# Diagonal blocks of the differential scores: a minimum on VectorE in place of mask products on TensorE

## The reference, cut to what matters

```
causal = key_pos[None, :] <= q_pos[:, None]
z = jnp.einsum('bhqcd,bhkcd->bhcqk', qi, k).astype(jnp.float32) * scale
z = jnp.where(causal, z, -jnp.inf)
probs = jax.nn.softmax(z, axis=-1)
a = probs[:, :, 0] - lam * probs[:, :, 1]
return jnp.einsum('bhqk,bhkd->bhqd', a.astype(v.dtype), v)
```

## Time and profile before

| | |
|---|---|
| median of the runs shown | 1189.08 us |
| the profiled execution's own time | 1189.23 us |
| its span | 1187.4 us |
| TensorE products, busy | 1177.8 us (99%) |
| TensorE weight loads, busy | 985.2 us (83%) |
| VectorE, busy | 830.1 us (70%) |
| ScalarE, busy | 719.6 us (61%) |
| GpSimd, busy | 95.8 us (8%) |
| products with `mask_df` | 16, from 284.1 to 916.1 us |
| granted clock of TensorE, mean | 0.999 |

### The profile page before, as it was taken

How to read it: one execution, slowest core, us unless ns; L and a number is a source line. 1 busy time by engine, 2 the same in 40 slices (tenths; PEclk the granted TensorE clock), 3 DMA queues, 4 the chain that set the end, 5 groups by cost and what they waited for, 6 DMA issues and landing times.

```text
span 1187.4 us, 17137 instructions
## 1 busy us (share of the span) xinstructions
PE 1177.8 (99%) x6032; PEld 985.2 (83%) x6032; DVE 830.1 (70%) x1198; ACT 719.6 (61%) x1162; POOL 95.8 (8%) x158
## 2 busy tenths in 40 slices
PE   9999999999999999999999999999999999999997
PEld 7888888888788888888888888878877888888886
DVE  6766767577667766676787776775766777767666
ACT  7655556766665755555685655576556666555554
POOL 5000001042000000000100000010600000000001
PEclk9999999999999999999999999999999999999999
DMA  8656565654345565656556555746343456556550
GB/s 286 220 184 205 178 212 181 198 175 139 113 174 177 178 207 182 203 171 218 177 167 205 174 198 187 242 160 213 121 148 132 168 177 211 178 178 209 180 194 36
DMA packets 138638, 215.36 MB, mean 181 GB/s; under 512 B 6942, under 2 KB 97888, under 8 KB 138592
## 3 DMA queue, kind: packets, MB, share of 16 engines
q1 hardware_dynamic: 135792, 208.43, 52.2%
q10 hardware_dynamic: 2576, 6.29, 1.7%
q0 software_dynamic: 224, 0.04, 0.0%
HBM read 213.68 MB, written 1.05 MB: 181 GB/s over the span
## 4 chain that ended last, share of the span: by engine, by line
PE 99%; DMA 0%; DVE 0%; ACT 0%; DVEq 0%; POOLq 0%; issue 0%; POOL 0%; ACTq 0%
PE ps L1544 22%; PE ps L1426 20%; PE ps L1428 19%; PE ps L1427 19%; PE ps L1554 12%; PE ps L1473 1%; PE ps L1645 1%; PE ps L1678 1%; PE ps L1691 1%; PE ps L1664 0%; PE ps L1651 0%; DMA soft<-in_p 0%; PE ps L1707 0%; PE ps L1704 0%; PE ps L1714 0%; PE ps L1722 0%
## 5 line engine op out<-in xcount | busy, mean ns | idle before, releaser
L1069 DVE SCALAR_TENSOR_TENSOR w_lo<-raw,g_layer,w_hi 128x512 fp32r<-128x512 f32 (+1 forms) x524 | 388.0, 800 | 139.3 <-ACT w_hi L632 138.6
L632 ACT ACTIVATE w_hi<-raw,g_layer 128x512 fp32r<-128x512 f32 (+1 forms) x524 | 346.9, 732 | 113.4 <-PE ps L1554 97.0
L1544 PE MATMUL ps<-x_both,w_hi 128*128 128x512 f32 x1152 | 287.7, 392 | 0.0
L1426 PE MATMUL ps<-w_hi,x_both 128*128 128x512 f32 x640 | 258.6, 404 | 0.1
L1428 PE MATMUL ps<-w_hi,x_both 128*128 128x512 f32 x640 | 250.5, 391 | 0.0
L1427 PE MATMUL ps<-w_lo,x_both 128*128 128x512 f32 x640 | 249.7, 390 | 0.0
L1544 PEld LDWEIGHTS ps<-x_both,w_hi 128*128 128x128 f32 x1152 | 209.3, 189 | 39.4 <-issue 0.3
L1066 DVE TENSOR_TENSOR w_lo<-raw,w_hi 128x1024 fp32r<-128x1024 f32 x114 | 134.7, 1222 | 55.3 <-ACT w_hi L629 55.3
L629 ACT ACTIVATE w_hi<-raw 128x1024 fp32r<-128x1024 f32 x114 | 114.7, 1052 | 91.9 <-PE ps L1428 91.8
L1554 PEld LDWEIGHTS ps<-x_both,w_lo 128*128 128x128 f32 x1152 | 152.6, 191 | 8.4
L1554 PE MATMUL ps<-x_both,w_lo 128*128 128x256 f32 x1152 | 156.0, 283 | 0.0
(11 more groups left out here) (216 smaller groups left out, 977.0 us busy)
## 6 DMA issues: line engine op xcount, KB each, us to landing
raw<-in_ffn_w_gu SPq DMA_DIRECT2D x170, 512.0 KB, 4.5
raw<-in_ffn_w_down SPq DMA_DIRECT2D x88, 512.0 KB, 3.9
raw<-in_w_in SPq DMA_DIRECT2D x80, 512.0 KB, 4.5
raw<-in_w_out SPq DMA_DIRECT2D x16, 512.0 KB, 4.0
raw<-in_w_ple_gate SPq DMA_DIRECT2D x16, 512.0 KB, 4.0
raw<-in_w_branch_sb SPq DMA_DIRECT2D x8, 512.0 KB, 3.7
raw<-in_w_branch_diff SPq DMA_DIRECT2D x8, 512.0 KB, 3.7
raw<-in_ffn_w_gu SPq DMA_DIRECT2D x12, 256.0 KB, 7.8
```

What stands on the lines that cost most here:

```text
L632: last = act.activation(w_hi[:, s, part], raw[:, s, part], ACT.Copy, scale=g_layer[:, g:g + 1])
L1069: last = dve.scalar_tensor_tensor(out=w_lo[:, s, part], in0=raw[:, s, part], scalar=g_layer[:, g:g + 1], in1=whi[:, part], op0=ALU.mult, o ...
L1426: pe.matmul(dst, x_h, w_h, start=first, stop=False, **group)
L1544: mm = pe.matmul(dst, w_hi[:, s, cols], x_both[:, :, 4 * half + k, :], start=half == 0 and k == 0, stop=stop and k == 3, skip_group_check= ...
```

## The change

The two mask products of each head are gone; the first score product of each bank now carries start=True and begins the bank. VectorE, once the scores are there, takes the elementwise minimum of the two diagonal blocks of each bank with a block of caps: 3.0e38 where the key may be seen, -1.0e30 where it may not. These are two instructions a head (one a bank) on 128x256 numbers, read from PSUM and written back in place. The maxima then wait for the second one by a semaphore of VectorE's own (`d_capped`). At the start GpSimd makes one 128x128 block of caps in float32 in place of two bf16 mask blocks.

```diff
-        mask_df = sb("mask_df", [P, SEQ], BF16)
+        cap_df = sb("cap_df", [P, 1, P])
...
-            pool.memset(mask_df[:, :], 0.0).then_inc(blank, 1)
+            pool.memset(cap_df[:, :, :], BIG).then_inc(blank, 1)
...
-
-                last = pool.affine_select(out=mask_df[:, c:c + P], in_=mask_df[:, c:c + P],
-                                          compare_op=ALU.is_ge, fill=NEG, base=0, pattern=[[-1, P]],
-                                          channel_multiplier=1)
-            last.then_inc(const_all, 1)
+            pool.affine_select(out=cap_df[:, 0, :], in_=cap_df[:, 0, :], compare_op=ALU.is_ge, fill=NEG, base=0,
+                               pattern=[[-1, P]], channel_multiplier=1).then_inc(const_all, 1)
...
                         dve.wait_ge(d_score, DF_HEADS * i + hd + 1)
+                        for c in range(2):
+                            last = dve.tensor_tensor(diagonal(DF_BANK[c]), diagonal(DF_BANK[c]),
+                                                     cap_df[:, :, :].to_broadcast([P, 2, P]), ALU.min)
+                        last.then_inc(d_capped, 1)
+                        dve.wait_ge(d_capped, DF_HEADS * i + hd + 1)
                         for t, (lo, hi) in enumerate(((0, P), (P, 384))):
                             last = dve.tensor_reduce(neg_max[:, t::2], ps[:, 6:8, lo:hi], AX_X, ALU.max, negate=True)
                         last.then_inc(d_max, 1)
...
-                for c in range(2):
-                    masked(DF_BANK[c], mask_df)
                 for c, rows in enumerate(HEAD_ROWS):
-                    pe.matmul(bank(DF_BANK[c])[:, 0:P], dfq_t[rows, hd, 0:P], dfk_t[rows, hd, 0:P], start=False,
+                    pe.matmul(bank(DF_BANK[c])[:, 0:P], dfq_t[rows, hd, 0:P], dfk_t[rows, hd, 0:P], start=True,
                               stop=False, skip_group_check=True)
```

More of the change, by code:

```diff
@@ L26 @@
 NEG = -1.0e30
+BIG = 3.0e38
 TT = SEQ // P
@@ L240, in trunk_kernel @@
         d_score = sem("d_score")
+        d_capped = sem("d_capped")
         d_max = sem("d_max")
```

## The result

The changed kernel takes 1192.61 us (median of 8 runs, 1192.47 to 1192.74) against 1189.05 us (8 runs, 1188.90 to 1189.27): +3.56 us, ratio 1.0030, 95% interval 1.0021 to 1.0038. The prediction was 1192.6. The profiled execution took 1192.47 us with a span of 1190.5. One execution of the second experiment took 2726 us and one of the kernel before beside it 3212 us, where the others took 1193 and 1189; the ratios leave both out.

A forecast was written before the change was run, and what follows sets the result against it. TensorE is 99% busy, but the prediction took the head-to-head chain across four engines to decide: D added per head, less absorption and freed masks, gives 2 x 1.76 = +3.5 us, 1192.6 us; range 1190.0 to 1195.0.

The forecast's parts named there:

- D: VectorE, each head: two minima and the wait start the maxima 0.78 us later; bounds 0.45 and 1.30.
- head 1, load for the values: TensorE, layer 0: the load waits for ScalarE's `mixed_t` and comes at 311.54 instead of 310.76, +0.78 us.
- head 2, load for the values: TensorE, layer 0: load comes at 326.85, in time for its product but no longer early, costing 0.10 us.
- head 3, load for the scores: TensorE, layer 0: load waits for the scaled output, at 331.02 instead of 330.15, +0.87 us.
- head 3, load for the turn: TensorE, layer 0: load waits for `mixed`, at 337.99 against 337.24 by its own pace; TensorE at +1.49 us.
- last turn, load: TensorE, layer 0: load waits for the scaled output, at 344.77 instead of 342.97; TensorE at +1.76 us.
- Where it is absorbed and where not: Layer 0's chain: head 0 absorbs D, its squares unmoved; later heads pass it on, TensorE ending +1.76 us.
- What is removed: TensorE: eight mask blocks at 0.32 us each give 2.6 us; bounds 0.21 and 0.42 a block.
- Twice 1.76 us: Both layers: each is 1.76 us later at its last turn, +3.5 us in all.
- the cover: Rival: minima fall in VectorE's idle time and TensorE keeps its 2.6 us, 1186.5 us; chance 0.07.
- The dearer minimum: Rival, VectorE: writing to PSUM makes D 1.0 to 1.3, +5.3 to +7.7 us, 1195.6 us; chance 0.11.
- less late: Rival: D nearer 0.5 or one more link TensorE had held, +0.5 to +2.3 us, some 1190.6; chance 0.22.

The follow-up runs named there:

- the second experiment: The kernel before with its masks kept on TensorE, and the two minima and their wait added on VectorE: 1193.24 us (ratio 1.0040).
- the three mended moves: Changed kernel with squares before the high pass's second half, earlier copies for heads 1 and 3, maxima between low-pass halves, `os_lo` before head 1's minima: 1186.31 us.
- the mended pair: The same mended moves on the changed kernel, 1186.31 us, and on the kernel before with masks on TensorE, 1188.47 us.

## Why the prediction was right, step by step

The trace after starts 0.34 us lower at the last product ahead of head 0's scores, where the mixing block has not changed yet (283.58 against 283.92, the fences below). The 0.34 us are there in the first 10 us, behind the first wait for the program's input, 0.41 us in this trace and 0.73 in the other; over the kernels above the same product stands anywhere from 283.09 to 283.92, so I count it as no part of the change. With 0.34 added to the times after:

| step | predicted | measured |
|---|---|---|
| minima and wait, D | 0.78 | 0.80 at head 0, 0.79 at head 1 |
| head 1, load for the values | 311.54 | 311.60 |
| head 2, load for the values | 326.85 | 326.92 |
| head 3, load for the scores | 331.02 | 331.13 |
| head 3, load for the turn | 337.99 | 338.06 |
| last turn, load | 344.77 | 344.82 |

The times fall 0.05 to 0.11 us behind the forecast ones. That the total agreed to 0.01 us is closer than its steps and luck in the last digit; the path is as forecast.

- *The addition D.* Right by the nearest row; a write to PSUM cost VectorE no more than one to SBUF (0.42 us, as `os_lo`). The rule of the Trainium skill (VectorE: DVE Perf Modes, The DRAIN you can't avoid) that a wait costs nothing extra gave 0.66 and +2.5 us; this case's trace does not agree: the maxima begin 0.04 us behind the second minimum's end (284.87 + 0.76 to 285.67), not 0.09 before it.
- *Where it is absorbed and where not.* Head 0 absorbs it, and with that its slack is used up; heads 1 to 3 do not. The experiment that puts the same time behind `mixed` and the one that keeps the masks both confirm it; that the whole loss is this chain is shown by the three mended moves, which take it away with the minima in place.
- *What is removed.* This term was mis-sized, with little effect on the total (by the prediction's own bounds 0.1 us or so). Predicted 0.32 us a block; measured 0.24 at head 0, where a product of the projection comes before (next start 0.31 behind it in place of 0.55), and 0.33 at head 1, where the values of the other attention do. The two fences are from before and after, TensorE at head 0 and the last product ahead of it in layer 1:

```profile
283.92 0.39 PE L1428 MATMUL ps<-w_hi,x_both 128*128 128x512 f32 x1
284.15 0.39 PE L1651 MATMUL ps<-mask_df,ident_b 128*128 128x256 bf16 x2
...
870.18 0.39 PE L1428 MATMUL ps<-w_hi,x_both 128*128 128x512 f32 x1
```

```profile
283.58 0.39 PE L1432 MATMUL ps<-w_hi,x_both 128*128 128x512 f32 x1
283.89 0.30 PEld L1706 LDWEIGHTS ps<-dfk_t,dfq_t 64*128 64x128 f32 x4 [0.35 <-issue]
...
871.60 0.39 PE L1432 MATMUL ps<-w_hi,x_both 128*128 128x512 f32 x1
```

  The load for 64 rows still starts late, 0.31 behind the product's start where 0.23 is the usual distance: 0.08 of the gap has moved to it. With the rule of TensorEngine Tiling (Array Packing), Tiling Modes, in the Trainium skill, this agrees in kind, though no run separates it from another cause; the price here is 0.08 us and not the 0.11 I had allowed. In the traces of the mended pair the four blocks of layer 0 are worth 0.24, 0.32, 0.23 and 0.25 us, 1.04 together; their times gave 2.16 for both layers.
- *Twice 1.76 us.* From layer to layer the distance is 586.26 us before (283.92 to 870.18) and 588.02 after (283.58 to 871.60): 1.76 us more, as in the sum. The last turn's load stands at +1.85, since it now starts with its product (both at 344.48) and not ahead of it (342.97, the product at 343.12); the product itself stands at +1.70. Two layers make 3.52 of the 3.56 us. The profiled executions differ by only 3.24, which with the 0.34 us of the start is 3.58.
- *The rivals.* Had the cover held, head 1's load would have come on time; it waited 1.81 us. The dearer minimum is excluded by its rows (0.42 us each, D 0.79), and the chain was not less late than forecast.

## What to carry to other kernels

Before moving work off the busiest engine, follow the order of time from one turn of the dependent loop to the next and mark where the loop waits for that engine; only there does added latency vanish, and only while nothing else is late does freed time count. A weight load that starts right behind another engine's end is the mark of a loop that is already as long as the work that covers it: what is added to such a loop is paid again in each turn that has no slack (here three of four). Then shorten the loop first, by putting the links ahead of independent work in each queue, and look at the loads again after each move, since a moved half of a pass stands in front of something else.

## What the runs showed of the hardware

VectorE's in-place minimum on PSUM costs what a subtraction of the same size from PSUM to SBUF does: 0.42 us at 128x256, 0.69 us at 128x512. Two bf16 mask products with their gap are worth 0.23 to 0.33 us by what stands before them, though their own rows look the same at every head.
